# Norm work between the two halves of each softmax step in a two-layer transformer and mixture-of-experts kernel

## The chip, the cores and the metric

The kernel runs on one core of one Trainium2 chip. The metric is the time of one execution on the device, in microseconds (us); the median of three runs is given. Everything is float32.

## What is computed

Two blocks follow each other. The change touches only the first, a transformer of two layers (l = 0, 1) of width 1024 with 256 latent tokens (x) and 256 context tokens (h_ctx). Cut to what matters:

```python
def merge_heads(attn, sgu, four, g_mix, w_out):
    a = rmsnorm(attn, g_mix[:ATTN_WIDTH])
    s = rmsnorm(sgu, g_mix[ATTN_WIDTH:ATTN_WIDTH + SGU_WIDTH])
    f = rmsnorm(four, g_mix[ATTN_WIDTH + SGU_WIDTH:])
    return jnp.concatenate([a, s, f], axis=-1) @ w_out
...
    c_attn = context_attention(cq, ck, cv, sink[l])            # layer 0 only
    yc = merge_heads(c_attn, c_sgu, c_four, g_mix[l], w_out[l])
...
    attn = latent_window_attention(q, k, v, ck, cv, sink[l])
    sgu = spatial_gating(jax.nn.gelu(u), jax.nn.gelu(gv), w_sgu[l], b_sgu[l], g_sgu[l])
    four = fourier_mix(f)
    y = merge_heads(attn, sgu, four, g_mix[l], w_out[l])
    x = x + g1 * rmsnorm(y, g_post_mix[l])
```

Each attention is a softmax with a sink over 8 heads. After it comes a squared-relu MLP of width 4096. The second block is a recurrent unit, gated linear attention in chunks, and a mixture of 32 experts of which each token takes 4.

## The kernel before, in words

Each engine runs its own program, written out by hand, and the engines meet at semaphores. TensorE (PE) multiplies into eight PSUM banks. PE's program takes the banks in turn (`take`): each product, mean, transpose or score takes the next one and waits until its last user has been read. Two scores of a step take an even bank and the one behind it, so the turn may skip one (`F.even`).

Sides are called C (context) and X (latent tokens); an attention is a pair (layer, side). There are three: (0, C), (0, X) and (1, X). Each has eight units, a unit being two heads' scores for 128 queries, and PE's `attention(l, s, i)` in step i issues the scores of unit i+1, the transposes of unit i-1 and the value products of unit i-2:

```python
                if i + 1 < 8:
                    scores(l, s, i + 1)
                if 0 <= i - 1 < 8:
                    turned(l, s, i - 1)
                if 0 <= i - 2 < 8:
                    values(l, s, i - 2)
```

VectorE (DVE) does the softmax in two halves. `soft_a` adds the band mask (X only, L1878), takes the maximum (L1880) and from it and the sink the exponentials' bias (L1881, L1882) and the sink's exponent (L1884). ScalarE (ACT) makes the exponentials with their sums (L1362, L1365), which also frees the scores' banks. `soft_b` of the unit before adds sum and sink, takes the reciprocal and scales the probabilities (L1891, L1892, L1895). PE transposes them (L572), ScalarE reads the transposes out (L1271), PE multiplies by the values (L586), ScalarE reads the result into CAT (L1271).

The three parts of the joint output, Fourier (mF, tiles 6 and 7 of CAT), gating (mS, 4 and 5) and attention (mA, 0 to 3), are each normed by a root mean square. ScalarE squares the tiles (`merge_squares`, L1299), POOL adds the squares (L2443), PE's `merge` multiplies by a constant to make the mean (L470, and L473 for the fourth square of mA), VectorE reads the mean into HOLD (L1795), ScalarE makes the reciprocal root as exp(-ln/2) (`root`, L1304, L1306), VectorE refines it by a Newton step (L1797 to L1799, with L1795 the function `rstd`) and scales the tiles by gain and root (L1909, the function `merge`). After that PE may multiply CAT by w_out (L607), one output tile per `w_out(l, s, n)`; ScalarE's `joined` reads the tile and squares it (L1271, L1376).

Among the steps of (0, C) stand PE's projections of the latent tokens (`w_in`, L497 to L508), which ScalarE reads, four of them through gelu; the gelu table and that of exp and ln displace each other on ScalarE (ACT_TABLE_LOAD). Among the steps of (0, X) stand the output tiles 0 to 5 of (0, C). Among those of (1, X) stand four products of the modulation (`ada`, L448), whose row ScalarE copies (`row`, L1271), PE transposes (`ada_turn`, L456) and VectorE adds up (L1778, L1780). Weights of all these are chunks of 2 MB in a ring, loaded by the SyncE queue when PE is through with the slot's last chunk; from the experts on the ring has eight slots.

## Time and profile before

| | |
|---|---|
| median of 3 runs | 2451.59 us (2449.55 to 2455.35) |
| profiled execution, its own time | 2454.41 us |
| its span, first to last instruction | 2452.5 us |
| mean granted TensorE clock | 0.982 of full |
| busy PE, DVE, ACT, POOL | 2310.3, 806.9, 487.8, 136.8 us |
| DMA | 601.61 MB, 245 GB/s on average |

The profile is one execution. Busy time counts an engine's own instructions, not the time in which it waits or issues. A wait is put down to the engine or DMA whose signal came last. The granted clock is the share of full TensorE speed that the chip allowed in a stretch; its two levels are 1.2 and 2.4 GHz, so a stretch at 0.9 was partly at the lower one. The three attention stages lie at about 128 to 197 us, 209 to 278 us and 803 to 865 us of the span.

### The profile page before, as it was taken

What the parts mean: (1) busy time and instruction counts of PE and PEld (TensorE: products, weight loads), DVE (VectorE), ACT (ScalarE), POOL (GpSimd) and SP (SyncE); (2) the same over time, 40 slices, a digit from 0 to 9 for tenths busy, and PEclk for the clock granted to TensorE, in tenths of its full rate; (3) what the DMA queues carried; (4) which work ended last, traced back from release to release, by engine and by line L of the source; (5) the groups of instructions that cost most, each with busy time, mean ns of one, the idle gap of its engine ahead of it and who ended that gap; (6) DMA issues with size and microseconds to landing.
All of it is one profiled execution on the core that took longest, in us unless ns stands there. A gap on an engine that the chain in (4) does not pass through costs nothing.

```text
span 2452.5 us, 34141 instructions
## 1 busy us (share of the span) xinstructions
PE 2310.3 (94%) x14422; PEld 1687.5 (69%) x14422; DVE 806.9 (33%) x2047; ACT 487.8 (20%) x1144; POOL 136.8 (6%) x138
## 2 busy tenths in 40 slices
PE   6888999999999789999999989999999999999997
PEld 3675788888887468887778854566566555555556
DVE  2044354577714520001665321222222222222223
ACT  2244330000013432100534120111111111111112
POOL 0000211134400000000000000000000000000000
PEclk9999999999999999999999999999999999999999
DMA  8910222124323433445233575899999999999991
GB/s 337 354 69 35 94 78 103 69 103 145 131 96 149 167 137 137 142 167 199 105 137 137 216 301 212 364 427 427 426 425 427 426 427 426 426 427 427 427 426 78
DMA packets 42115, 601.61 MB, mean 245 GB/s; under 512 B 4672, under 2 KB 5184, under 8 KB 5600
## 3 DMA queue, kind: packets, MB, share of 16 engines
q1 hardware_dynamic: 41472, 593.30, 59.8%
q10 hardware_dynamic: 480, 5.97, 0.6%
q8 instruction: 122, 2.00, 0.3%
q14 instruction: 41, 0.34, 0.0%
HBM read 598.20 MB, written 1.05 MB: 244 GB/s over the span
## 4 chain that ended last, share of the span: by engine, by line
PE 81%; DMA 13%; DVE 2%; ACT 2%; issue 1%; POOL 0%; SPq 0%; POOLq 0%; PEldq 0%; ACTq 0%; DVEq 0%
PE PS L1095 14%; PE PS L854 7%; PE PS L1119 7%; DMA RG<-in_w_up 7%; PE PS L633 7%; PE PS L668 6%; PE PS L617 6%; PE PS L720 5%; DMA BIG<-in_w_up 4%; PE PS L508 4%; PE PS L607 3%; PE PS L706 2%; PE PS L1028 2%; PE PS L1131 2%; PE PS L564 2%; DMA RG<-in_w_ada 1%
## 5 line engine op out<-in xcount | busy, mean ns | idle before, releaser
L2318 DVE TENSOR_SCALAR STAT<-PS 128x128 f32<-128x128 f32 (+1 forms) x128 | 37.8, 296 | 683.1 <-PE PS L1095 683.1
L1095 PE MATMUL PS<-BIG,XS 128*64 128x256 f32 (+1 forms) x2016 | 239.8, 388 | 8.3 <-DMA BIG<-in_w_up 8.0
L1095 PEld LDWEIGHTS PS<-BIG,XS 128*64 128x64 f32 (+1 forms) x2016 | 146.4, 139 | 99.8 <-issue 20.4
L1095 PE MATMUL PS<-RG,XS 128*64 128x256 f32 (+1 forms) x1520 | 180.2, 387 | 10.1 <-DMA RG<-in_w_up 10.1
L1271 ACT ACTIVATE BIG<-PS 128x256 f32<-128x256 f32 (+2 forms) x205 | 86.5, 430 | 515.1 <-PE PS L633 138.9
L854 PE MATMUL PS<-XS,RG 128*128 128x256 f32 x768 | 172.1, 382 | 5.0 <-DVE XS L1822 4.1
L1095 PEld LDWEIGHTS PS<-RG,XS 128*64 128x64 f32 (+1 forms) x1520 | 108.9, 139 | 80.4 <-DMA RG<-in_w_up 15.9
L854 PEld LDWEIGHTS PS<-XS,RG 128*128 128x128 f32 x768 | 145.6, 191 | 26.7 <-issue 6.9
L1678 ACT ACTIVATE STAT<-STAT 128x128 f32<-128x128 f32 (+1 forms) x128 | 40.1, 313 | 585.5 <-DVE STAT L2318 585.5
L617 PE MATMUL PS<-HN,RG 128*128 128x256 f32 x640 | 140.3, 382 | 4.0 <-ACT HN L1316 4.0
L1795 DVE TENSOR_SCALAR HOLD<-PS 128x256 f32<-128x256 f32 x27 | 11.4, 423 | 401.6 <-PE PS L484 299.8
L617 PEld LDWEIGHTS PS<-HN,RG 128*128 128x128 f32 x640 | 122.4, 192 | 21.4 <-issue 4.6
L1119 PE MATMUL PS<-BIG,CAT 128*64 128x256 f32 (+1 forms) x992 | 120.9, 387 | 0.1
L720 PE MATMUL PS<-BIG,RG 128*128 128x256 f32 x512 | 110.7, 379 | 0.0
L508 PE MATMUL PS<-HN,RG 128*128 128x256 f32 x448 | 103.6, 387 | 5.6 <-ACT HN L1316 3.4
L720 PEld LDWEIGHTS PS<-BIG,RG 128*128 128x128 f32 x512 | 97.3, 190 | 13.2
L1119 PEld LDWEIGHTS PS<-BIG,CAT 128*64 128x64 f32 (+1 forms) x992 | 73.6, 139 | 42.5 <-issue 10.0
L508 PEld LDWEIGHTS PS<-HN,RG 128*128 128x128 f32 x448 | 85.6, 194 | 22.3 <-issue 7.6
L607 PE MATMUL PS<-CAT,RG 128*128 128x256 f32 x384 | 87.8, 388 | 0.3 <-DVE CAT L1909 0.3
L1119 PE MATMUL PS<-RG,CAT 128*64 128x256 f32 x768 | 86.4, 381 | 0.4 <-DVE CAT L2327 0.4
L2443 POOL TENSOR_TENSOR HN<-HN 128x256 f32<-128x256 f32 x60 | 45.9, 765 | 732.9 <-ACT HN L1299 315.2
L607 PEld LDWEIGHTS PS<-CAT,RG 128*128 128x128 f32 x384 | 74.0, 194 | 12.2 <-DVE CAT L1909 1.0
(347 smaller groups left out, 3310.3 us busy)
## 6 DMA issues: line engine op xcount, KB each, us to landing
BIG<-in_w_up SPq DMA_DIRECT2D x64, 2048.0 KB, 30.3
RG<-in_w_up SPq DMA_DIRECT2D x48, 2048.0 KB, 30.4
RG<-in_w_ff SPq DMA_DIRECT2D x32, 2048.0 KB, 8.1
BIG<-in_w_down SPq DMA_DIRECT2D x32, 2048.0 KB, 31.2
RG<-in_w_ada SPq DMA_DIRECT2D x24, 2048.0 KB, 8.9
RG<-in_w_down SPq DMA_DIRECT2D x24, 2048.0 KB, 34.2
RG<-in_w_in SPq DMA_DIRECT2D x23, 2048.0 KB, 8.0
SM<-in_w_up SPq DMA_DIRECT2D x16, 2048.0 KB, 30.6
```

The costliest lines, as they stand in the source:

```text
L508: m = pe.matmul(banks[b][:, 0:256], w[:, k, c0:c0 + 128], N[:, k, :], start=k == 0, stop=k == 7)
L564: pe.matmul(banks[b][:, 0:wd], Q[s][:, j, qb * 128:qb * 128 + 128], KZ[:, hf, 512 - wd:512], start=True, stop=True).then_inc(s_full[b], 1)
L607: m = pe.matmul(banks[b][:, 0:256], w[:, k, 128 * (n % 4):128 * (n % 4) + 128], own(CAT, s)[:, k, :], start=i == 0, stop=i == 7)
L617: m = pe.matmul(banks[b][:, 0:256], w[:, k, 128 * n:128 * n + 128], own(HN, s)[:, k, :], start=k == 0, stop=k == 7)
L633: m = pe.matmul(banks[b][:, 0:256], w[:, k, :], a[:, k, :], start=not first and k == 0, stop=k == 3, skip_group_check=True)
L668: return pe.matmul(banks[b[j]][:, 256 * half:256 * half + 256], w, a, start=first and half == 0, stop=last, skip_group_check=True)
L706: m = pe.matmul(banks[b[s, o]][:, 0:256], w[:, k, 128 * o:128 * o + 128], own(FFH, s)[:, 16 * h + k, :], start=h + k == 0, stop=h * 16 + k ...
L720: m = pe.matmul(banks[b][:, 0:256], w[:, k, :], own(FFH, s)[:, k, :], start=k == 0, stop=k == 31)
L854: m = pe.matmul(banks[b][:, 0:256], w[:, k, 128 * n:128 * n + 128], src[:, k, 0:256], start=k == 0, stop=k == 7)
L1095: i = pe.matmul(half_of(b, h, sides), Xg[:, k, 0:cap], w[:, k, h * wd:h * wd + wd], start=False, stop=k == 7)
L1119: m = pe.matmul(half_of(b, h, sides), T_[:, k, :], w[:, k, h * wd:h * wd + wd], start=k == 0, stop=k == 7)
L1271: i = act.activation(dst, banks[b][rows, part], fn)
```

## The change

The norm's pieces and some neighbours take other places in the steps. Nothing is computed otherwise, and each engine has the same instructions.

- On VectorE `rstd` is split into `mean_read` and `refined`, and `merge` ends with `scaled`. In the three attentions the pieces stand between `soft_a` and `soft_b` of a step, one step apart: mean in one, refinement in the next, scaling in the one after. For (0, C) these are steps 3 to 7 of the attention (i = 5 to 9 of the loop), for both X steps 3 to 7. The mA norm of (0, C), which stood ahead of `gated(0, X)`, is spread over steps 0 to 2 of (0, X).
- On PE the means of mF and mS stand ahead of the step's scores instead of behind its values, for X one step earlier by number (3 and 5, not 4 and 6). The mA mean of (0, C) moves from ahead of gating to behind the first scores of (0, X).
- On ScalarE `attention` is split into `exponentials` and `read_outs`; the roots stand between them, and so do the output tiles (`joined`, of one step later) and the modulation rows (`row`, which now reads the product of PE's step before instead of waiting for that of the same step).
- On VectorE `turned` stands between the halves, one step later.

The core of the diff (lines that only mirror these are left out):

```diff
@@ -750,23 +750,23 @@
                     scores(0, C, 0)
                 if 1 <= i <= 5:
                     rotate(0, i - 1)
-                if i >= 2:
-                    attention(0, C, i - 2)
                 if i == 5:
                     merge("mF", 0, C)
                 if i == 7:
                     merge("mS", 0, C)
+                if i >= 2:
+                    attention(0, C, i - 2)
             fourier_d(0, X)
-            merge("mA", 0, C)
             gating(0, X)
             fourier_t(0, X)
             scores(0, X, 0)
+            merge("mA", 0, C)
             for i in range(10):
+                if i == 3:
+                    merge("mF", 0, X)
+                if i == 5:
+                    merge("mS", 0, X)
                 attention(0, X, i)
-                if i == 4:
-                    merge("mF", 0, X)
-                if i == 6:
-                    merge("mS", 0, X)
                 if 2 <= i < 8:
                     w_out(0, C, i - 2)
             w_out(0, C, 6)
...
@@ -1349,7 +1349,7 @@
                 for j in range(2):
                     evac(own(CAT, s)[:, 6 + j, :], ("four", l, s, j))
-            def attention(l, s, i):
+            def exponentials(l, s, i):
                 wd = 512 if s == X else 256
                 if i < 8:
                     u, par = units(l, s) + i, i % 2
@@ -1363,6 +1363,9 @@
                                        accum_out=dn[:, hf:hf + 1]).then_inc(s_free[b], 1)
                     act.wait_ge(s_es, u + 1)
                     act.activation(es, nm, ACT.Exp).then_inc(s_ex, 1)
+
+            def read_outs(l, s, i):
+                wd = 512 if s == X else 256
                 if 0 <= i - 1 < 8:
                     for hf in range(2):
                         evac(PT[:, (i - 1) % 2, hf, 0:wd], ("t", l, s, i - 1, hf), part=slice(0, wd))
@@ -1452,26 +1455,30 @@
                     merge_squares("mF", 0, C)
                     merge_squares("mS", 0, C)
                 if i >= 2:
-                    attention(0, C, i - 2)
+                    exponentials(0, C, i - 2)
                 if i == 5:
                     root(("mF", 0, C), C, 0)
                 if i == 7:
                     root(("mS", 0, C), C, 1)
+                if i >= 2:
+                    read_outs(0, C, i - 2)
...
-            root(("mA", 0, C), C, 2)
             fourier_t(0, X)
             merge_squares("mF", 0, X)
             merge_squares("mS", 0, X)
             for i in range(10):
-                attention(0, X, i)
-                if i == 4:
+                exponentials(0, X, i)
+                if i == 0:
+                    root(("mA", 0, C), C, 2)
+                if i == 3:
                     root(("mF", 0, X), X, 0)
-                if i == 6:
+                if i == 5:
                     root(("mS", 0, X), X, 1)
-                if 2 <= i < 8:
-                    joined(0, C, i - 2)
+                if 3 <= i < 9:
+                    joined(0, C, i - 3)
+                read_outs(0, X, i)
...
             for i in range(10):
-                attention(1, X, i)
-                if i == 4:
+                exponentials(1, X, i)
+                if 1 <= i <= 4:
+                    row(1, 5 + i)
+                if i == 3:
                     root(("mF", 1, X), X, 0)
-                if i == 6:
+                if i == 5:
                     root(("mS", 1, X), X, 1)
-                if i <= 3:
-                    row(1, 6 + i)
+                read_outs(1, X, i)
...
-            def rstd(key, eps, s=0, slot=0):
+            def mean_read(key, eps, s=0):
+                b = full(("ms",) + key)
+                dve.tensor_scalar(HOLD[:, 256 * s:256 * s + 256], banks[b][:, 0:256], eps, None, ALU.add).then_inc(s_free[b], 1)
+
+            def refined(key, s=0, slot=0):
                 r, me, tm = stat(s, slot), HOLD[:, 256 * s:256 * s + 256], HOLD[:, 512 + 256 * s:768 + 256 * s]
-                b = full(("ms",) + key)
-                dve.tensor_scalar(me, banks[b][:, 0:256], eps, None, ALU.add).then_inc(s_free[b], 1)
                 dve.wait_ge(s_root, ROOT[key] + 1)
                 step(dve.tensor_tensor(tm, r, r, ALU.mult))
                 step(dve.scalar_tensor_tensor(tm, tm, -0.5, me, ALU.mult, ALU.mult))
                 step(dve.scalar_tensor_tensor(r, tm, 1.5, r, ALU.add, ALU.mult))
                 return r
+
+            def rstd(key, eps, s=0, slot=0):
+                mean_read(key, eps, s)
+                return refined(key, s, slot)
...
-            def attention(l, s, i):
-                if i < 8:
-                    soft_a(l, s, i)
-                if 0 <= i - 1 < 8:
-                    soft_b(l, s, i - 1)
+            SLOT = {"mF": 0, "mS": 1, "mA": 2}
+
+            def scaled(part, l, s, ks=None):
+                gm = s1(f"g_mix{l}")
+                for k in ks or PARTS[part]:
+                    ck = own(CAT, s)[:, k, :]
+                    dve.scalar_tensor_tensor(ck, ck, gm[:, k:k + 1], stat(s, SLOT[part]), ALU.mult, ALU.mult).then_inc(s_mt, 1)
 
             def merge(part, l, s):
-                slot = ("mF", "mS", "mA").index(part)
-                r = rstd((part, l, s), 1e-6, s, slot)
-                gm = s1(f"g_mix{l}")
-                for k in PARTS[part]:
-                    ck = own(CAT, s)[:, k, :]
-                    dve.scalar_tensor_tensor(ck, ck, gm[:, k:k + 1], r, ALU.mult, ALU.mult).then_inc(s_mt, 1)
+                rstd((part, l, s), 1e-6, s, SLOT[part])
+                scaled(part, l, s)
...
+                if 2 <= i < 10:
+                    soft_a(0, C, i - 2)
+                if i == 5:
+                    mean_read(("mF", 0, C), 1e-6, C)
+                if i == 6:
+                    refined(("mF", 0, C), C, 0)
+                if i == 7:
+                    scaled("mF", 0, C)
+                    mean_read(("mS", 0, C), 1e-6, C)
+                if i == 8:
+                    refined(("mS", 0, C), C, 1)
+                if i == 9:
+                    scaled("mS", 0, C)
+                if 3 <= i < 11:
+                    soft_b(0, C, i - 3)
                 if i <= 5:
                     rope(0, i - 1)
-                if i == 5:
-                    merge("mF", 0, C)
-                if i == 7:
-                    merge("mS", 0, C)
             value_norm(0, X)
-            merge("mA", 0, C)
             gated(0, X)
             for i in range(10):
-                attention(0, X, i)
+                if i < 8:
+                    soft_a(0, X, i)
+                if i == 0:
+                    mean_read(("mA", 0, C), 1e-6, C)
+                if i == 1:
+                    refined(("mA", 0, C), C, 2)
+                    scaled("mA", 0, C, (0, 1))
+                if i == 2:
+                    scaled("mA", 0, C, (2, 3))
+                if i == 3:
+                    mean_read(("mF", 0, X), 1e-6, X)
                 if i == 4:
-                    merge("mF", 0, X)
+                    refined(("mF", 0, X), X, 0)
+                if i == 5:
+                    scaled("mF", 0, X)
+                    mean_read(("mS", 0, X), 1e-6, X)
                 if i == 6:
-                    merge("mS", 0, X)
+                    refined(("mS", 0, X), X, 1)
+                if i == 7:
+                    scaled("mS", 0, X)
+                if 1 <= i < 9:
+                    soft_b(0, X, i - 1)
             merge("mA", 0, X)
             post("mix", 0, C)
             prenorm("ff", 0, C)
@@ -2084,13 +2121,23 @@
             value_norm(1, X)
             gated(1, X)
             for i in range(10):
-                attention(1, X, i)
+                if i < 8:
+                    soft_a(1, X, i)
+                if 2 <= i <= 5:
+                    turned(1, 4 + i)
+                if i == 3:
+                    mean_read(("mF", 1, X), 1e-6, X)
                 if i == 4:
-                    merge("mF", 1, X)
+                    refined(("mF", 1, X), X, 0)
+                if i == 5:
+                    scaled("mF", 1, X)
+                    mean_read(("mS", 1, X), 1e-6, X)
                 if i == 6:
-                    merge("mS", 1, X)
-                if 1 <= i <= 4:
-                    turned(1, 5 + i)
+                    refined(("mS", 1, X), X, 1)
+                if i == 7:
+                    scaled("mS", 1, X)
+                if 1 <= i < 9:
+                    soft_b(1, X, i - 1)
```

Where the rows stand now. VectorE in the middle of the attention (0, X), first before: `soft_b`, then the whole mF norm (L1795 to L1909), then the next `soft_a`.

```order
L1891 TENSOR_TENSOR MISC<-MISC 128x2
L1892 RECIPROCAL MISC<-MISC 128x2
L1895 TENSOR_SCALAR BIG<-BIG,MISC 128x512 x2
L1795 TENSOR_SCALAR HOLD<-PS 128x256
L1797 TENSOR_TENSOR HOLD<-STAT 128x256
L1798 SCALAR_TENSOR_TENSOR HOLD<-HOLD 128x256
L1799 SCALAR_TENSOR_TENSOR STAT<-HOLD,STAT 128x256
L1909 SCALAR_TENSOR_TENSOR CAT<-CAT,SM,STAT 128x256 x2
L1878 TENSOR_TENSOR PS<-PS,SM 128x2x128
L1880 TENSOR_REDUCE MISC<-PS 128x2
L1881 SCALAR_TENSOR_TENSOR MISC<-MISC,SM 128x2
L1882 TENSOR_SCALAR MISC<-MISC 128x2
```

The same place in the changed kernel, where `mean_read` is L1802, `refined` L1807 to L1809, `soft_a` L1892 to L1898 and `soft_b` L1905 to L1909:

```order
L1802 TENSOR_SCALAR HOLD<-PS 128x256
L1905 TENSOR_TENSOR MISC<-MISC 128x2
L1906 RECIPROCAL MISC<-MISC 128x2
L1909 TENSOR_SCALAR BIG<-BIG,MISC 128x512 x2
L1892 TENSOR_TENSOR PS<-PS,SM 128x2x128
L1894 TENSOR_REDUCE MISC<-PS 128x2
L1895 SCALAR_TENSOR_TENSOR MISC<-MISC,SM 128x2
L1896 TENSOR_SCALAR MISC<-MISC 128x2
L1898 TENSOR_TENSOR MISC<-SM,MISC 128x2
L1807 TENSOR_TENSOR HOLD<-STAT 128x256
L1808 SCALAR_TENSOR_TENSOR HOLD<-HOLD 128x256
L1809 SCALAR_TENSOR_TENSOR STAT<-HOLD,STAT 128x256
```

The mean's read has moved ahead of a `soft_b`, the three refining instructions have a whole `soft_b` and `soft_a` between themselves and the read, and the scaling follows a step later.

PE between the attentions (0, C) and (0, X), as a piece of the difference (L523 is the first Fourier product, L546 gating, L534 the second Fourier product):

```order
@@ -86,6 +86,4 @@
 L586 MATMUL PS<-BIG 64x128 x4
 L523 MATMUL PS<-SM,BIG 128x256 x4
-L470 MATMUL PS<-HN,MISC 128x256
-L473 MATMUL PS<-HN,MISC 128x256
 L546 MATMUL PS<-SM,BIG 64x128 x8
 L534 MATMUL PS<-SM,BIG 128x256
```

The two matmuls of the mA mean are gone from ahead of gating. They come back behind the first scores (L564) of the next attention:

```order
@@ -97,6 +95,14 @@
 L534 MATMUL PS<-SM,BIG 128x256
 L535 MATMUL PS<-SM,BIG 128x256
-L564 MATMUL PS<-BIG 128x512 x6
+L564 MATMUL PS<-BIG 128x512 x2
+L470 MATMUL PS<-HN,MISC 128x256
+L473 MATMUL PS<-HN,MISC 128x256
+L564 MATMUL PS<-BIG 128x512 x4
 L572 MATMUL PS<-SM,BIG 128x128 x8
```

ScalarE in the attention (1, X), first before: the modulation row (L1271, SM) stands behind the read-outs and ahead of the next exponentials (L1362).

```order
L1271 ACTIVATE BIG<-PS 128x512 x2
L1271 ACTIVATE SM<-PS 128x512
L1362 ACTIVATE BIG,MISC<-PS,MISC 128x512 x2
L1365 ACTIVATE MISC<-MISC 128x2
L1271 ACTIVATE BIG<-PS 128x512 x2
L1271 ACTIVATE CAT<-PS 128x128
L1271 ACTIVATE SM<-PS 128x512
```

Now it stands right behind the exponentials, and the root (L1304, L1306) too:

```order
L1271 ACTIVATE BIG<-PS 128x512 x2
L1271 ACTIVATE CAT<-PS 128x128
L1362 ACTIVATE BIG,MISC<-PS,MISC 128x512 x2
L1365 ACTIVATE MISC<-MISC 128x2
L1271 ACTIVATE SM<-PS 128x512
L1304 ACTIVATE STAT<-HOLD 128x256
L1306 ACTIVATE STAT<-STAT 128x256
L1271 ACTIVATE BIG<-PS 128x512 x2
```

The read-outs of transposes (BIG) and values (CAT) now come last in a step.

## Rows read from the trace of the kernel before

**Rows 1.** The page, parts 1 and 4: busy time; chain that ended last
```profile
PE 2310.3 (94%) x14422; PEld 1687.5 (69%) x14422; DVE 806.9 (33%) x2047; ACT 487.8 (20%) x1144; POOL 136.8 (6%) x138
...
PE 81%; DMA 13%; DVE 2%; ACT 2%; issue 1%; POOL 0%; SPq 0%; POOLq 0%; PEldq 0%; ACTq 0%; DVEq 0%
```

**Rows 2.** Windows: length, busy PE, PEld, DVE, ACT, POOL (counts), clock, DMA share, GB/s
```profile
152.37:192.84 40.47, 32.16 (x155) 24.92 (x153) 15.52 (x51) 22.65 (x51) 0.00 (x0) 0.87 0.15 53
...
209.43:223.07 13.64, 11.61 (x49) 6.24 (x47) 10.22 (x26) 8.49 (x24) 1.45 (x2) 0.87 0.00 0
223.07:277.61 54.54, 47.92 (x278) 35.39 (x276) 20.81 (x59) 22.55 (x60) 3.62 (x5) 0.91 0.11 40
...
802.53:833.28 30.75, 27.68 (x185) 13.67 (x184) 17.33 (x51) 15.83 (x43) 1.72 (x2) 1.00 0.71 262
833.28:867.77 34.49, 18.44 (x127) 12.93 (x126) 16.44 (x47) 13.33 (x36) 1.44 (x2) 0.80 0.03 11
```

**Rows 3.** Waits of PE, 127 to 210: total us, times, longest
```profile
PE PS L564 <- ACT BIG L1362: 4.9, 2, 2.4
PE PS L470 <- POOLq L2446: 3.1, 1, 3.1
```

**Rows 4.** Waits of PE, 209 to 288, same columns
```profile
PE PS L572 <- DVE BIG L1895: 5.4, 2, 3.3
```

**Rows 5.** Waits of PE, 802 to 873, same columns
```profile
PE PS L564 <- ACT BIG L1362: 9.6, 3, 6.5
PE PS L572 <- DVE BIG L1895: 6.8, 1, 6.8
PE PS L470 <- POOLq L2446: 2.8, 1, 2.8
```

**Rows 6.** Timeline, DVE, B: start, length, line, tiles, [idle before]
```profile
238.99 0.42 DVE L1795 TENSOR_SCALAR HOLD<-PS 128x256 f32<-128x256 f32 x1 [6.96 <-PE PS L470]
240.34 0.42 DVE L1797 TENSOR_TENSOR HOLD<-STAT 128x256 f32<-128x256 f32 x1 [0.93 <-ACT STAT L1306]
...
241.72 0.88 DVE L1909 SCALAR_TENSOR_TENSOR CAT<-CAT,SM,STAT 128x256 f32<-128x256 f32 x2
242.52 0.43 DVE L1878 TENSOR_TENSOR PS<-PS,SM 128x256 f32<-128x256 f32 x1
```

**Rows 7.** Timeline, PE, B: scores after the norm of step 4
```profile
245.56 3.75 PE L564 MATMUL PS<-BIG 128*128 128x512 f32 x4 [3.16 <-ACT BIG L1362]
```

**Rows 8.** Timeline, PE, B: scores, transposes, output tile, next scores
```profile
226.63 1.88 PE L564 MATMUL PS<-BIG 128*128 128x512 f32 x4
228.38 1.32 PE L572 MATMUL PS<-SM,BIG 128*128 128x128 f32 x8
...
230.66 3.72 PE L607 MATMUL PS<-CAT,RG 128*128 128x256 f32 x16
234.22 1.88 PE L564 MATMUL PS<-BIG 128*128 128x512 f32 x4
```

**Rows 9.** Timeline, PE, C: transposes, later scores
```profile
815.09 1.04 PE L572 MATMUL PS<-SM,BIG 128*128 128x128 f32 x8
...
821.13 1.96 PE L564 MATMUL PS<-BIG 128*128 128x512 f32 x4 [1.54 <-ACT BIG L1362]
```

**Rows 10.** Timeline, start of B: DVE soft_a(1), soft_b(0); PE first transposes
```profile
213.55 0.43 DVE L1878 TENSOR_TENSOR PS<-PS,SM 128x256 f32<-128x256 f32 x1
...
215.75 0.15 DVE L1891 TENSOR_TENSOR MISC<-MISC 128x2 f32<-128x2 f32 x1
...
216.78 1.52 PE L572 MATMUL PS<-SM,BIG 128*128 128x128 f32 x8 [2.03 <-DVE BIG L1895]
```

**Rows 11.** Timeline, ACT, A: table load ahead of exponentials
```profile
156.42 1.28 ACT L1309 ACT_TABLE_LOAD   x1
```

**Rows 12.** Timeline, ACT, C: read-out of a modulation row
```profile
819.72 0.60 ACT L1271 ACTIVATE SM<-PS 128x512 f32<-128x512 f32 x1 [2.24 <-PE PS L448]
```

**Rows 13.** Windows, experts, columns as in rows 2
```profile
1560.00:1878.00 318.00, 316.77 (x2770) 193.14 (x2766) 71.60 (x257) 35.91 (x90) 0.00 (x0) 1.00 1.01 427
```

10 lines of the change are left out of this document (4 added, 6 removed).

## The prediction

> **What bounds the kernel now.** I read the page first: TensorE (PE) is busy for 94% of the span and carries 81% of the chain that ended last [rows 1]. A step that is moved is worth something only where PE stands still or runs slowly, so I cut the span at the three attention stages with the view by windows [rows 2]. Stage A (context tokens of layer 0, among the input projections of the latent tokens) has 8.3 us of idle PE in 40.5; the start of stage B (latent tokens, layer 0) 2.0 in 13.6; B's steady steps 6.6 in 54.5; stage C (layer 1) 3.1 in 30.8 and then 16.1 in 34.5. The clock column tells the rest: 0.80 to 0.91 where PE idles, 1.00 where it doesn't. I write the lower clock's cost as excess: busy time above what the same matmuls take at the full level.
>
> The waits say who is late. In A: the scores' banks, freed by ScalarE's exponentials; in the passage from A to B 3.1 us for the POOL sums of the attention part's norm [rows 3]. In B: transposes that wait for VectorE's scaled probabilities [rows 4], and once scores that wait for exponentials. In C the same two, longer, and the POOL sum again [rows 5]. The timeline of B shows how that comes about. PE makes the norm's mean; VectorE reads it at 238.99, then stands still for 0.93 us until ScalarE has made the root, refines it, scales two tiles and only at 242.52 begins the next softmax, whose scores had been ready [rows 6]. ScalarE's exponentials are late by as much, and PE's next scores find their bank occupied: 3.16 us idle, and the scores then take 3.75 us at the lower of the two clock levels (1.2 GHz), against 1.88 at 2.4 GHz [rows 7, 8].
>
> **Stage B, steady steps.** The change gives the norm's mean, refinement and scaling to three different steps, behind the maximum of a softmax (soft_a) and ahead of the normalisation of the one before (soft_b); PE makes the mean ahead of the scores of its step. VectorE then never waits for the root: ScalarE makes it one step earlier. What is added ahead of soft_b is 0.42 us (mean), 1.4 (three refining instructions, 240.34 to 241.72) or 0.84 (two tiles) [rows 6]. A step on PE lasts 7.6 us from one output tile to the next [rows 8]; VectorE's own work in it is 2.2 for soft_a (213.55 to 215.75) and 1.2 for soft_b (1.03 from its start to the first transposes, and the second tile) [rows 10], so up to 1.4 more still leaves it 2.8 us early. ScalarE reads output tile n one step later than before, so the exponentials no longer stand behind a tile that PE ends last in the step. The banks turn in the same eight; I followed each take and found one place in B where a wait remains, about 0.4 us for the last values. PE's work at the full level: six output tiles at 3.56 (230.66 to 234.22) are 21.4, four scores at 1.75 (226.63 to 228.38) are 7.0, six transposes at 1.0 are 6.0, seven values at 1.0 are 7.0, two means 1.1 [rows 8, 9]. That is 42.5, with the wait 42.9, against 54.5: **11.6 us**. Lower end: only the 6.6 idle goes and the excess stays; upper end 12.
>
> **Passage and start of B.** The attention part's mean is moved from ahead of gating to behind the first scores. The 3.1 us wait for POOL [rows 3] is then covered by gating and the Fourier products, save that gating itself waits for VectorE's value norm, which ends about when PE gets there; with the mean's own matmuls out of the way gating starts 3.3 us earlier. But VectorE had done this norm behind gating and Fourier, in nobody's way. Now it stands in the start of the softmax: read 0.42, refinement 1.4, two of the four tiles 0.84, together 2.66, all ahead of soft_b(0). The first transpose, which came right on the heels of that soft_b [rows 10], comes 2.6 us later after its scores. What is left is 3.3 - 2.6 = **0.7 us**. The other two tiles stand ahead of soft_b(1) and are hidden by the scores that PE has in between. PE now stands still for about 3.7 us in one piece at the first transpose, where it stood 2.0, and the clock in that window was already 0.87 [rows 2], so I keep its excess as it was. The Trainium skill (TensorE: Matmul & The Clock Gate, What's actually happening) says that the throttled state is the default and that sustained activity releases it; by that rule the longer idle piece speaks against this change and would cost some 2 us more at the start, a sum of 26.5 in place of 28.5. The trace agrees as far as the slow scores behind the 3.16 us wait go [rows 7]; no row shows this very place. Ends: -2 to +3.
>
> **Stage A.** From step 6 on each step waits for one chain: projection, gelu read-out, table load 1.28 us [rows 11], exponentials. The order of these isn't touched, so these waits stay; the softmax that was late through the norm in steps 6 and 8 was covered by this chain in any case. Two things change. The scores now mostly find a bank that isn't the previous scores' one, so PE does 0.9 us of scores before it waits and meets the wait at the transpose; and the mean of step 5 fills a wait of 0.6. Against that soft_b(2) comes 0.3 late behind the mean's read. Walking steps 5 to 10 gives 7.9 us of waits where there were 8.3 and half a microsecond less in step 5: **0.7 us**. Ends: -1.5; +6 if the excess (0.13 of 40.5, so 5.3) went too.
>
> **Stage C.** Here the read-out of a modulation row stood at the end of ScalarE's step, behind PE's last product; the next exponentials stood behind it [rows 12], and PE's scores waited 1.54 twice [rows 9]. It now stands between exponentials and read-outs and reads the product of the step before. With the two norms (6.5 and 6.8 us of idle, most of [rows 5]) treated as in B, PE's work is: eight scores 14.4, eight transposes 8.0, eight values 8.1, four row products 7.4, four turns 2.4, two means 1.1, together 41.4. Waits that I still find: 0.3 at the scores of step 5, 1.1 at the transpose of step 6, 2.2 at that of step 7 (no row products fill these steps, and VectorE's 2.2 + 0.84 + 1.2 is longer than PE's work), 0.3, and the POOL sum's 2.8, which isn't touched. That is 48.1, and 1.6 for the clock behind the waits: 49.7 against 65.2, **15.5 us**. Lower end 9 (a microsecond or two of wait in each of four steps and half the excess kept), upper end 17.
>
> No instruction is added or taken away, no DMA is moved in its queue, and the weights' slots come free relative to PE as before. **Sum:** 0.7 + 0.7 + 11.6 + 15.5 = 28.5. Is it kept to the end? From 1560 us on, the experts' weights stream at 427 GB/s without a gap [rows 13], and later PE waits for them (most of the 13% of DMA in the chain [rows 1]). But this stream can only start when PE gives back the slots of the first experts, after everything above; it moves forward with PE. The profiled execution took 2454.41 us; less 28.5 it is 2425.9. The median of the runs is 2.8 below the profiled one, so the forecast for the median is **2423 us**.
>
> **Rivals.**
> First, half of it: the moved pieces stand ahead of soft_b, and a mean must have come from PE before soft_b may run. If each norm step costs a microsecond of wait for VectorE and the excess stays in B and C, B gives 6.6, C 10, the rest nothing: 2451.6 - 16.6 = 2435. For it: VectorE's margin comes from hand-walked steps, and in C it is gone from step 6 on. Against: in B the margin is 2.8 us in steps of 7.3.
> Second, nothing arrives: the weight stream bounds the end and the gain ends as waiting for it, 2451.6. For it: the stream is saturated [rows 13]. Against: its start is tied to PE.
> Third, slower, through the clock. New short waits at the transposes, one in most steps, with the 3.7 us at B's start could hold PE at the 1.2 GHz level across steps that ran at 2.4. B and C hold 42.5 + 41.4 = 83.9 us of work at the full level, which doubles at the lower one; once more than a third of it (28.5) runs there, the gain is gone. Half of it there gives 2423 + 42 = 2465. For it: A shows 0.87 with waits of about 2 us in each step. Against: B keeps almost no wait, and C's first half shows 1.00 with two waits of 1.5. The rule of the Trainium skill cited above would work through this mechanism.
>
> **How the numbers follow.** The forecast with its bounds 0.72, half 0.20, nothing 0.03, slower 0.03, and 0.02 for a gain above the upper ends. All lower ends together give 12, all upper ones 38; both at once are unlikely. From 2414 to 2438 holds the forecast's spread and most of the half case. A measurement of this kernel tells about 0.2%, 5 us, from no change: faster 0.94, within it 0.03, slower 0.03.
>
> **What would show it.** In the profile after: B's steady part near 43 us with clock near 1.00 and no idle PE behind L1362 or soft_b; C near 50; the POOL wait of the passage gone and a wait of 3 to 4 us at B's first transpose in its place; A unchanged within 2. VectorE's 0.93 us wait for the root is gone in B and C, and the stream's full rate starts some 28 us earlier. Wrong would be: scores that still wait for exponentials in B, the clock of B below 0.95, or soft_b behind a mean that PE hasn't made.

## The result, and the profile of the changed kernel

| | before | changed |
|---|---|---|
| median | 2452.80 us (4 runs, 2449.55 to 2455.35) | 2423.02 us (4 runs, 2419.32 to 2425.50) |
| ratio, 95% interval | | 0.9884, 0.9872 to 0.9896 |
| profiled execution: own time, span | 2454.41, 2452.5 us | 2425.50, 2423.6 us |
| mean granted TensorE clock | 0.982 | 0.983 |

The forecast was 2423 us. Its sum was made against the profiled execution and gave 2425.9 for it; 2425.5 was measured. Two executions, one of the kernel before (11141.6 us, granted clock 0.202) and one of the sums alone below (3473.11 us, 0.651), are left out of everything below. The terms did not all come out as well as their sum, so I take them one by one. The cuts are starts of PE instructions, the same in every kernel. A: first scores of (0, C) to the first Fourier product. Passage: from there to the first scores of (0, X). Start of B: from there to the first output tile. B: first to seventh output tile. C: first scores of (1, X) to the mean of its attention part.

| us | before | changed | gained | predicted |
|---|---|---|---|---|
| A | 69.45 | 66.43 | 3.0 | 0.7 |
| passage + start of B | 12.35 + 13.64 | 7.43 + 17.45 | 1.1 | 0.7 |
| B, steady steps | 54.54 | 42.20 | 12.3 | 11.6 |
| C | 65.25 | 49.07 | 16.2 | 15.5 |
| all the rest, code unchanged | 2237.3 | 2241.0 | -3.7 | 0 |

The last line is a surprise: the same instructions lasted 3.7 us longer. It is taken up below. Each column is one execution, and the other kernels' profiles show that the lengths of A, of the passage, of the start, of B and of C also differ from one execution to the next; the part on the prediction gives each gain with that spread.

Windows of the changed kernel. In order: A, the start of B, B, C up to the end of the scores of step 5, the rest of C, and the same stretch of the experts as in [rows 13]. Columns as in [rows 2].

```profile
129.31:195.74 66.43, 59.34 (x320) 47.84 (x318) 30.44 (x99) 32.17 (x88) 1.97 (x2) 0.95 0.18 64
203.17:220.62 17.45, 13.74 (x54) 7.91 (x52) 13.77 (x36) 9.11 (x26) 1.45 (x2) 0.80 0.00 0
220.62:262.82 42.20, 42.11 (x278) 33.16 (x277) 20.38 (x57) 21.80 (x60) 3.63 (x5) 1.00 0.15 51
789.42:820.17 30.75, 30.59 (x194) 15.05 (x193) 23.57 (x69) 18.85 (x52) 1.72 (x2) 1.00 0.73 271
820.17:838.49 18.32, 12.69 (x118) 9.80 (x117) 9.97 (x30) 9.91 (x27) 1.44 (x2) 0.91 0.02 6
1560.00:1878.00 318.00, 316.77 (x2772) 192.93 (x2770) 72.63 (x261) 36.21 (x91) 0.00 (x0) 1.00 1.01 426
```

The third line, against that of [rows 2] which begins at 223.07, is the core of the change. PE was busy for 47.92 of 54.54 us at 0.91 and is now busy for 42.11 of 42.20 at 1.00: 6.5 us of idle time and 5.8 of excess are gone. Not all of the excess was the clock: a clock of 0.91 over 54.54 us is some 5 us lost, idle time included. The experts' stream is as dense as in [rows 13]. It starts earlier with PE: from the first expert product to the end it is 1017.25 us, against 1016.97.

Waits of PE in the changed kernel, 203 to 275 us:

```profile
PE PS L572 <- DVE BIG L1909: 3.7, 1, 3.7
PE PS L484 <- ACT HN L1379: 0.5, 1, 0.5
```

The same view, 789 to 850 us, to be held against [rows 5]:

```profile
PE PS L572 <- DVE BIG L1909: 2.8, 2, 2.1
PE PS L470 <- POOLq L2493: 2.8, 1, 2.8
PE PS L607 <- DVE CAT L1917: 1.6, 1, 1.6
PE PS L564 <- ACT BIG L1362: 0.2, 1, 0.2
```

No wait is left in B's steps. What is left at its start is the 3.7 us that the prediction put there. C's list is the predicted one, a little shorter, and one more: 1.6 at the first output tile.

VectorE in B, one norm spread over three steps:

```profile
224.81 0.42 DVE L1802 TENSOR_SCALAR HOLD<-PS 128x256 f32<-128x256 f32 x1 [4.07 <-PE PS L470]
225.15 0.15 DVE L1905 TENSOR_TENSOR MISC<-MISC 128x2 f32<-128x2 f32 x1
...
228.73 0.42 DVE L1807 TENSOR_TENSOR HOLD<-STAT 128x256 f32<-128x256 f32 x1
...
233.79 0.43 DVE L1892 TENSOR_TENSOR PS<-PS,SM 128x256 f32<-128x256 f32 x1 [2.42 <-PE PS L564]
...
235.99 0.87 DVE L1917 SCALAR_TENSOR_TENSOR CAT<-CAT,SM,STAT 128x256 f32<-128x256 f32 x2
```

The 0.93 us wait for the root of [rows 6] is gone: the mean is read at 224.81, the refinement comes 3.9 us later. VectorE now waits for scores (2.42), where PE's scores used to wait behind it [rows 7].

PE in the changed kernel, the start of B and two steps:

```profile
213.06 1.94 PE L572 MATMUL PS<-SM,BIG 128*128 128x128 f32 x8 [3.71 <-DVE BIG L1909]
214.79 3.62 PE L564 MATMUL PS<-BIG 128*128 128x512 f32 x4
...
226.32 1.04 PE L572 MATMUL PS<-SM,BIG 128*128 128x128 f32 x8
227.29 1.09 PE L586 MATMUL PS<-BIG 128*64 128x128 f32 x16
228.32 3.72 PE L607 MATMUL PS<-CAT,RG 128*128 128x256 f32 x16
231.87 1.88 PE L564 MATMUL PS<-BIG 128*128 128x512 f32 x4
```

From one step's transposes to the next step's it is now 7.3 us, with PE busy throughout. The scores at 214.79 take twice the 1.88 of those at 231.87: behind the 3.71 us of idle time PE is at the lower clock level for a while.

### The profile page after: what moved, and what is told of

It reads as the page before. It is cut to its first block, busy times and chain, and to the rows that moved or that the text cites. A ratio compares the mean times of both kernels' runs of the same rounds, so it can differ in the third digit from the quotient of the medians.

```text
span 2423.6 us, 34147 instructions
## 1 busy us (share of the span) xinstructions
PE 2301.6 (95%) x14422; PEld 1683.5 (69%) x14422; DVE 806.4 (33%) x2047; ACT 486.2 (20%) x1144; POOL 136.9 (6%) x138
## 4 chain that ended last, share of the span: by engine, by line
PE 81%; DMA 13%; DVE 2%; ACT 2%; issue 1%; POOL 0%; SPq 0%; POOLq 0%; PEldq 0%; ACTq 0%; DVEq 0%
PE PS L1095 14%; PE PS L854 8%; PE PS L1119 7%; DMA RG<-in_w_up 7%; PE PS L633 7%; PE PS L668 6%; PE PS L617 6%; PE PS L720 5%; DMA BIG<-in_w_up 4%; PE PS L508 4%; PE PS L607 3%; PE PS L706 2%; PE PS L1028 2%; PE PS L1131 2%; PE PS L448 1%; DMA RG<-in_w_ada 1%
## 5 line engine op out<-in xcount | busy, mean ns | idle before, releaser
L1095 PE MATMUL PS<-BIG,XS 128*64 128x256 f32 (+1 forms) x2016 | 239.9, 388 | 8.4 <-DMA BIG<-in_w_up 8.3
L1095 PEld LDWEIGHTS PS<-BIG,XS 128*64 128x64 f32 (+1 forms) x2016 | 146.7, 139 | 99.7 <-issue 20.5
L1095 PE MATMUL PS<-RG,XS 128*64 128x256 f32 (+1 forms) x1520 | 181.0, 388 | 9.8 <-DMA RG<-in_w_up 9.8
L1271 ACT ACTIVATE BIG<-PS 128x256 f32<-128x256 f32 (+2 forms) x205 | 85.9, 430 | 508.4 <-PE PS L633 138.9
L1095 PEld LDWEIGHTS PS<-RG,XS 128*64 128x64 f32 (+1 forms) x1520 | 109.1, 139 | 80.2 <-issue 16.1
L1802 DVE TENSOR_SCALAR HOLD<-PS 128x256 f32<-128x256 f32 x27 | 11.4, 423 | 383.7 <-PE PS L484 299.9
```

Source lines behind the costliest of these rows:

```text
L1095: i = pe.matmul(half_of(b, h, sides), Xg[:, k, 0:cap], w[:, k, h * wd:h * wd + wd], start=False, stop=k == 7)
L1271: i = act.activation(dst, banks[b][rows, part], fn)
```

## The experiments

Each kernel was run beside the kernel before on the same chip; its segments are cut as above. "The change" is the changed kernel. Line numbers differ from kernel to kernel.

### The parts one by one

Each stage's part of the diff was put into the kernel before on its own. First **C alone**: all hunks for (1, X) on the three engines, of which this is PE's.

```diff
             for i in range(10):
+                if i == 3:
+                    merge("mF", 1, X)
+                if i == 5:
+                    merge("mS", 1, X)
                 attention(1, X, i)
-                if i == 4:
-                    merge("mF", 1, X)
-                if i == 6:
-                    merge("mS", 1, X)
```

> The kernel before with the change in the attention (1, X) alone. If the gain of each stage is its own waits (theory), stage C takes 49 us instead of 65 and the whole is about 16 us (0.66%) faster than before; A, passage and B are as before. If the gain came from the clock recovering over the whole first block, C alone would keep part of its waits' excess and give under 10 us.

2433.64 us, ratio 0.9934 (0.9917 to 0.9950), C 47.52 us at a clock of 1.00. The gain is C's own, as expected. **B alone**, the same hunks for (0, X) with the output tiles on ScalarE, without the mA norm of (0, C):

```diff
-                if 2 <= i < 8:
-                    joined(0, C, i - 2)
+                if 3 <= i < 9:
+                    joined(0, C, i - 3)
+                read_outs(0, X, i)
```

> The kernel before with the change in the steps of the attention (0, X) alone; the mA norm of (0, C) and stage C stay. Theory: the steady part of B 42 to 43 us instead of 54.5, its start 13.6 as before, about 12 us (0.49%) faster. Rival (clock): with the slow clock of stage A in front, the steady part would stay above 46.

2441.56 us, ratio 0.9961 (0.9951 to 0.9971), B 42.21 us, so the clock in front of it doesn't hold it up. **A alone**, the hunks for (0, C):

```diff
-                if i >= 2:
-                    attention(0, C, i - 2)
                 if i == 5:
                     merge("mF", 0, C)
                 if i == 7:
                     merge("mS", 0, C)
+                if i >= 2:
+                    attention(0, C, i - 2)
```

> The kernel before, with the change made in the steps of (0, C) alone. Theory: A's gain of the change (3.0 us by the segment where 0.7 was predicted) is one of its own: A 66.4 or 64.9 in place of 69.5, B and C as before (54.5 and 65.3), 3 us faster by the span, some 2449. Rival: A's length differs between executions by steps of about 1.5 us whatever the kernel, and half of the gain is such a step; then A here comes out at 67.9 and the time at 2450.5.

2448.26 us, ratio 0.9987 (0.9977 to 0.9997), A 66.43 us, to the hundredth the length that it has in the change. The three ratios fall short of 1 by 0.66%, 0.39% and 0.13%, together 1.18%; the change falls short by 1.16%. So the parts add up as far as the intervals tell (together about 0.2%, 5 us), and what is moved between A and B (the mA norm) is worth no more than that. The prediction's 0.7 for A was too small.

Windows of A, first of the kernel before, then of A alone:

```profile
127.63:197.08 69.45, 60.56 (x320) 49.08 (x318) 30.54 (x99) 32.35 (x88) 1.97 (x2) 0.93 0.17 61
```

```profile
126.48:192.91 66.43, 59.33 (x321) 47.84 (x319) 30.46 (x99) 32.16 (x88) 1.97 (x2) 0.95 0.18 64
```

Idle time went from 8.9 to 7.1 us, busy time from 60.6 to 59.3: 1.8 and 1.2 us. The idle time is a property of the code: it is 8.9 in all six profiles whose code of A is that of the kernel before, and 7.1 in all eight with the change. The busy time is not: A took 69.5 us in three of the six and 67.7 to 67.9 in the other three, and 66.4 in three of the eight and 64.9 in five.

### The attention part's norm at the start of B

The change with the mA norm of (0, C) where it was before:

```diff
             fourier_d(0, X)
+            merge("mA", 0, C)
             gating(0, X)
             fourier_t(0, X)
             scores(0, X, 0)
-            merge("mA", 0, C)
```

> The changed kernel with the mA norm of (0, C) put back on all three engines: ahead of gating. Theory: passage 12.3 us (7.4 in the change) and B's start 13.6 (17.5), so about 1 us slower than the change, that is nearly the same: what the passage gains the start gives back. Rival: moving the norm was a clear part of the gain, 3 us or more.

2423.81 us, ratio 0.9884 (0.9868 to 0.9901), the same as the change. The passage is 12.33, the start of B 13.63 us, as before, with the waits that were there before. Its waits from 195 to 225 us:

```profile
PE PS L470 <- POOLq L2486: 3.1, 1, 3.1
PE PS L572 <- DVE BIG L1908: 2.0, 1, 2.0
```

Against this profile the passage of the change gains 4.9, and its start gives back 3.8. Both numbers hold a piece of clock that belongs to the execution. Here are the passage and the start in C alone, which has the norm in the same place:

```profile
195.24:205.96 10.72, 7.61 (x46) 6.11 (x45) 5.33 (x14) 4.21 (x12) 1.45 (x2) 1.00 0.55 196
205.96:218.71 12.75, 10.12 (x50) 5.31 (x48) 11.66 (x30) 8.51 (x24) 1.56 (x2) 1.00 0.00 0
```

The wait for POOL is the same 3.1 us, and yet the passage takes 10.72 in place of 12.35 us. B alone and the three kernels below that move the row, the sums or both have the same two lengths.

Then the change with only the mean's read ahead of `soft_b`, refinement and scaling behind it (VectorE, (0, X)):

```diff
                 if i == 0:
                     mean_read(("mA", 0, C), 1e-6, C)
-                if i == 1:
-                    refined(("mA", 0, C), C, 2)
-                    scaled("mA", 0, C, (0, 1))
-                if i == 2:
-                    scaled("mA", 0, C, (2, 3))
...
                 if 1 <= i < 9:
                     soft_b(0, X, i - 1)
+                if i == 1:
+                    refined(("mA", 0, C), C, 2)
+                if i == 2:
+                    scaled("mA", 0, C)
```

> The changed kernel with the refinement and the scaling of the mA norm of (0, C) behind soft_b of steps 1 and 2 instead of ahead of it; its mean's read stays. Theory: the 3.7 us wait of the first transpose falls to about 1.5, B's start takes 14 to 15 us instead of 17.5, the whole is about 3 us faster than the change. Rival (PE's start is bound by the scores and the exponentials, not by soft_b): start stays at 17.

2421.42 us, ratio 0.9886 (0.9869 to 0.9902), not told from the change. Start of B 15.48 us, where 14 to 15 were expected. PE's timeline of this kernel says why:

```profile
207.31 1.06 PE L572 MATMUL PS<-SM,BIG 128*128 128x128 f32 x8 [1.54 <-DVE BIG L1909]
212.07 1.17 PE L572 MATMUL PS<-SM,BIG 128*128 128x128 f32 x8 [1.98 <-DVE BIG L1909]
```

The first wait is 2.2 us shorter, as expected, but the second transposes now wait 1.98: the refinement behind `soft_b(0)` delays the next `soft_a`. Together they are 3.5 us, only 0.2 less than before the move; most of the difference to 17.45 is the clock (0.93 in this window, 0.80 in the change's), and other profiles of the change's code at this place show 16.09. VectorE has little room at this start (busy for 13.77 us of 17.45 in the change's second window above), so a piece that is moved off one wait lands in the next.

### "Between the halves" or "a step apart"?

The change does two things at once. **In one piece**: the whole norm stands between the halves, in one step (both X):

```diff
                 if i == 3:
-                    mean_read(("mF", 0, X), 1e-6, X)
-                if i == 4:
-                    refined(("mF", 0, X), X, 0)
+                    merge("mF", 0, X)
                 if i == 5:
-                    scaled("mF", 0, X)
-                    mean_read(("mS", 0, X), 1e-6, X)
-                if i == 6:
-                    refined(("mS", 0, X), X, 1)
-                if i == 7:
-                    scaled("mS", 0, X)
+                    merge("mS", 0, X)
```

> The changed kernel, but in both X attentions VectorE does mean, wait for the root, refinement and scaling of mF in step 3 and of mS in step 5 in one piece, ahead of soft_b. Theory (what counts is that VectorE doesn't wait for the root with a softmax behind it): about 3 us more per norm in B and for mF in C, so steady part of B 48 us, C 52, about 9 us slower than the change. Rival (PE's and ScalarE's new order does it all): B and C within 1 us of the change.

2435.52 us (2 runs), ratio 0.9926 (0.9897 to 0.9954); B 50.33, C 54.84, both 2 to 3 us more than expected. VectorE and then PE in B:

```profile
222.65 0.42 DVE L1807 TENSOR_TENSOR HOLD<-STAT 128x256 f32<-128x256 f32 x1 [0.93 <-ACT STAT L1306]
```

```profile
225.84 1.06 PE L572 MATMUL PS<-SM,BIG 128*128 128x128 f32 x8 [2.88 <-DVE BIG L1909]
...
244.29 1.59 PE L572 MATMUL PS<-SM,BIG 128*128 128x128 f32 x8 [3.30 <-DVE BIG L1909]
```

The 0.93 us for the root is back, the norm's 3.6 us (0.42 + 0.93 + 1.4 + 0.84) stand in one piece ahead of the scaled probabilities, and PE pays twice. The run doesn't tell the wait for the root from the 2.7 us of work that now also stand in one step; no run splits the work but keeps the wait, or the other way round. **Behind `soft_b`**: the pieces a step apart as in the change, but all behind `soft_b`:

```diff
+                if 1 <= i < 9:
+                    soft_b(0, X, i - 1)
                 if i == 3:
                     mean_read(("mF", 0, X), 1e-6, X)
...
                 if i == 7:
                     scaled("mS", 0, X)
-                if 1 <= i < 9:
-                    soft_b(0, X, i - 1)
```

> The changed kernel with the pieces still a step apart, but behind soft_b instead of between the halves. Theory: a step apart is what counts; B unchanged at 42.2 us, C 0.5 to 1.5 us shorter, since the transposes of steps 6 and 7 no longer wait for refinement and scaling. Rival (between the halves is what counts): B and C each 2 us or more longer.

2424.51 us (2 runs), ratio 0.9881 (0.9852 to 0.9910); B 42.20, C 46.75. Its waits from 784 to 846 us:

```profile
PE PS L470 <- POOLq L2493: 2.8, 1, 2.8
PE PS L572 <- DVE BIG L1909: 2.3, 1, 2.3
PE PS L564 <- ACT BIG L1362: 0.2, 1, 0.2
```

In whole times as fast as the change, to within the 0.3% of the interval. In B the idle time of PE is 6.6 us in the kernel before, 6.3 in one piece and 0.1 a step apart, on either side of `soft_b`: there the spacing of the pieces is what gains, and the rest of the new order gives next to nothing without it. In C it is one of three gains. The idle time is 19.1 us in the kernel before, 15.8 with rows and sums moved (both, below), 9.8 in one piece, 5.8 in the change and 5.3 behind `soft_b`. Besides rows and sums, the step to 9.8 holds PE's earlier means, ScalarE's new order and the place between the halves, which no run takes apart in C.

### The output tiles

The change with ScalarE's read-out of output tile n back at the end of its own step:

```diff
                 if i == 5:
                     root(("mS", 0, X), X, 1)
-                if 3 <= i < 9:
-                    joined(0, C, i - 3)
                 read_outs(0, X, i)
+                if 2 <= i < 8:
+                    joined(0, C, i - 2)
```

> The changed kernel with the output tiles' read-out on ScalarE back at the end of the step that makes the tile. Theory: the exponentials stand behind it again and the second bank of the scores is freed late: 0.1 to 0.3 us in each of some five steps, steady part of B 43 to 44 us instead of 42.2. Rival: no difference, since VectorE's soft_b ends later anyway.

B 46.62 us, 4.4 more than in the change and more than the 43 to 44 expected. PE's timeline, and the window of B:

```profile
220.26 1.95 PE L564 MATMUL PS<-BIG 128*128 128x512 f32 x4 [1.25 <-ACT BIG L1362]
...
237.03 1.96 PE L564 MATMUL PS<-BIG 128*128 128x512 f32 x4 [1.25 <-ACT BIG L1362]
...
253.71 1.09 PE L586 MATMUL PS<-BIG 128*64 128x128 f32 x16 [0.72 <-ACT BIG L1362]
```

```profile
214.85:261.47 46.62, 43.29 (x278) 32.80 (x276) 21.00 (x59) 21.71 (x60) 3.63 (x5) 1.00 0.13 46
```

The exponentials stand behind a tile that PE ends last in the step. Of the 4.4 us, 3.2 are these waits. The other 1.2 are busy time (43.29 us, where the same matmuls take 42.11 in the change) and not the clock, which is at 1.00 throughout; two groups of transposes last 1.33 us in place of 1.04, and the rest stays open. Two runs of the whole kernel (2426.56 us, ratio 0.9889, 0.9860 to 0.9918) do not tell it from the change; the segment does.

### The two waits of 1.5 us in C's first half

The prediction gave them to ScalarE's read-out of the modulation row alone. Into the kernel before went first only that move, **the row alone**:

```diff
                 exponentials(1, X, i)
+                if 1 <= i <= 4:
+                    row(1, 5 + i)
                 read_outs(1, X, i)
...
-                if i <= 3:
-                    row(1, 6 + i)
```

> The kernel before, with only the modulation rows of stage C on ScalarE moved from the end of the step to behind the exponentials, and so reading the product of the step before. Theory: the two waits of 1.54 us of the scores go and nothing else, stage C 62 us instead of 65.2. Rival: the waits are the exponentials' own and stay.

2450.95 us, ratio 0.9998 (0.9986 to 1.0010). The expectation failed: both waits stayed, at 1.53 us each. VectorE in this kernel:

```profile
813.50 0.19 DVE L1784 TENSOR_REDUCE MODT<-PS 128x8 f32<-128x32 f32 x1 [2.48 <-PE PS L456]
813.72 0.17 DVE L1786 TENSOR_TENSOR MODT<-MODT,SM 128x8 f32<-128x8 f32 x1
813.80 0.43 DVE L1890 TENSOR_TENSOR PS<-PS,SM 128x256 f32<-128x256 f32 x1
```

The sums of the turned row (the function `turned`, the first two rows) stand ahead of the next `soft_a` (the third) and wait for PE's turn, which comes late in the step. The scores were ready meanwhile. The change had moved these sums as well, and the prediction names them nowhere. So **the sums alone** and **both**:

```diff
                 if i < 8:
                     soft_a(1, X, i)
+                if 2 <= i <= 5:
+                    turned(1, 4 + i)
...
-                if 1 <= i <= 4:
-                    turned(1, 5 + i)
```

> The kernel before, with VectorE's sums of the turned row alone moved behind soft_a, a step later; ScalarE's row stays at the end of the step. Theory that both stand in the way (ScalarE's row waits for PE's last product of the step and holds the next exponentials, VectorE's sums hold soft_a): the waits of 1.5 us stay, at most a few tenths shorter, C 64.5 to 65.3. Theory that VectorE alone was in the way: they go, C 62 to 63.

2450.68 us (9 runs), ratio 1.0003 (0.9993 to 1.0013), both waits at 1.54. ScalarE in this kernel: the row waits for PE's last product, and the exponentials behind it start at 814.47, although VectorE's bias for them was ready at 811.6.

```profile
813.97 0.60 ACT L1271 ACTIVATE SM<-PS 128x512 f32<-128x512 f32 x1 [2.24 <-PE PS L448]
814.47 0.68 ACT L1362 ACTIVATE BIG<-PS,MISC 128x512 f32<-128x512 f32 x1
815.04 0.20 ACT L1362 ACTIVATION_READ_ACCUMULATOR BIG<-PS,MISC 128x1 f32 x1
```

> The kernel before, with the modulation row's read-out moved behind the exponentials and VectorE's sums of the turned row moved behind soft_a, a step later (in (1, X) only; norms and everything else as before). Theory: the two waits of 1.5 us in C's first half came from VectorE, which stood behind PE's turn at the end of a step and so began soft_a late; they go, C is 62 to 63 in place of 65.3, the rest unchanged: 2.5 to 3 us faster, some 2448.5. Rival (the row on ScalarE alone, as the prediction had it): already refuted by the row alone; then C would stay at 65. If both are needed, neither alone gives anything, and this one does.

2446.43 us (10 runs), ratio 0.9984 (0.9974 to 0.9995). C is 61.83 and the two waits are gone; ScalarE's row now waits behind the exponentials:

```profile
812.36 0.69 ACT L1362 ACTIVATE BIG<-PS,MISC 128x512 f32<-128x512 f32 x1
...
814.66 0.60 ACT L1271 ACTIVATE SM<-PS 128x512 f32<-128x512 f32 x1 [0.76 <-PE PS L448]
```

Neither move alone gives anything, both together 3.4 us of C: two engines were late by the same amount for the same scores, each hidden by the other.

### A version that takes the remaining waits too

The change, with refinement and scaling of the mA norm of (0, C) and of the mS norm of (1, X) behind `soft_b`, and C's output tiles begun with the four tiles of CAT that are ready. PE:

```diff
+            w_out_first(1, X, 0)
+            w_out_first(1, X, 1)
             merge("mA", 1, X)
-            for n in range(8):
+            w_out_first(1, X, 2)
+            for n in range(3):
+                w_out_rest(1, X, n)
+            for n in range(3, 8):
                 w_out(1, X, n)
```

> The change, and besides: refinement and scaling of the mA norm of (0, C) behind soft_b of steps 1 and 2; in (1, X) refinement and scaling of the mS norm behind soft_b of steps 6 and 8; and the products with w_out of the first three output tiles of (1, X) begun with the four tiles of CAT that are ready, two of them ahead of the mA mean and one behind it, finished when the attention's tiles are scaled. Theory: start of B 1 to 2 us shorter (15.5 in place of 17.5), C's steps 1 to 2 shorter, and the waits of 2.8 (POOL's sum) and 1.6 (VectorE's scaling) at C's end filled with 5.3 us of matmuls that were due anyway: another 3 to 4. Together 5 to 7 us faster than the change, some 2417. Rival (the waits' place is taken by the lower clock or by the next wait of VectorE, the root of mA): 1 to 3 us, some 2421.

2419.56 us (4 runs), ratio 0.9857 (0.9835 to 0.9879). PE at C's end in this kernel:

```profile
830.14 3.72 PE L606 MATMUL PS<-CAT,RG 128*128 128x256 f32 x16
833.70 0.59 PE L470 MATMUL PS<-HN,MISC 128*128 128x256 f32 x2
...
834.56 1.89 PE L606 MATMUL PS<-CAT,RG 128*128 128x256 f32 x8
838.03 5.45 PE L614 MATMUL PS<-CAT,RG 128*128 128x256 f32 x24 [1.58 <-DVE CAT L1939]
```

The 2.8 us wait for POOL is filled. The 1.58 for VectorE's scaling stays: it follows the mean, wherever the mean stands. From C's first scores to the mean of the joint squares (L482) it is 75.9 us; 79.5 in the change, 77.9 in the kernel with the mA norm behind `soft_b`, whose code of C is the change's own, and 77.3 in the one with all pieces behind it. So this end gains 2.0 to 3.6 us over the change, by the execution, and 1.4 over that one; 3 to 4 from filling and 1 to 2 from the steps were expected. The whole kernel's interval overlaps the change's, so it is the fastest median here but not shown to be faster.

## Why the prediction was right

**B, 11.6 predicted, 12.3 measured.** Every step held: the means one step ahead, no wait for the root, no scores behind a tile, 42.20 us where 42.9 were built up from durations. The 0.4 us wait that I had found did not show. The experiment with the output tiles bears out that they are part of it. One reservation: B in the kernel before is not always 54.54. In the row alone and the sums alone, which don't touch it, it was 51.69 and 51.68, with the same 6.6 us of idle time and a clock of 0.97; in A alone, C alone and both it was 54.5. With the change it is 42.2 in four profiles. B alone brought 0.39% (0.29 to 0.49), which is 9.6 us. The gain lies between 9.5 and 12.3, by the execution. A second reservation: the prediction read the excess as the clock alone. Of its 5.8 us the clock accounts for some 5 at most; the rest is something else, as in the experiment with the output tiles.

**C, 15.5 predicted, 16.2 measured.** The predicted waits 0.3, 1.1, 2.2, 0.3 and 2.8 came as 0.16, 0.76, 2.08, none and 2.79, and its 41.4 us of work as 41.7 in C alone, at a clock of 1.00. The 1.6 for the clock is an affair of the execution: 1.5 in the change's profile, nothing in C alone and in the kernel with the mA norm behind `soft_b`, where C is 47.52. So the gain is 16.2 to 17.7. The step that fails is the attribution of the two waits of 1.54: "It now stands between exponentials and read-outs" is true of ScalarE's row, but the row alone gives nothing. VectorE's sums had to be moved too. The sum came out since it was built from PE's work with all waits taken out, not from the reasons for them. The 1.6 at the first output tile lies behind the cut of C, and was 0.3 before. PE does 8 matmuls ahead of it, in 1.89 us now; before, at the lower level, in 3.15, which covered the difference.

**A, 0.7 predicted, 3.0 measured.** Mis-sized twice. Idle time fell by 1.8 us, where the prediction's own terms give 0.4 + 0.5: the wait of step 5 went from 0.59 to 0.15, two waits of 2.44 at the scores became waits of 1.49 at the transposes, and one of 1.49 became 2.01. The clock term, which I had left at zero, is 1.2 between these two profiles. By the lengths given under A alone the gain is anywhere from 1.3 to 4.6 us between two executions, and 2.8 to 3.1 between the longer lengths of each kind as well as between the shorter ones; A alone brought 0.13% (0.03 to 0.23), 3.2 us. That it belongs to this part is settled, its clock share is not.

**Passage and start of B, 3.3 - 2.6 = 0.7 predicted, 4.9 - 3.8 = 1.1 measured.** The first transposes came 9.9 us behind the first scores instead of 7.35 (209.43 to 216.78): 2.5 later, as predicted. The rest of the difference is the clock, and mostly the execution's. Where the old passage ran at 1.00 it took 10.72 us with the same wait, so at the full level the passage gains 3.3, the predicted number, and the further 1.6 is not the change's doing. The start of B took 13.64 us in three profiles without the change and 12.75 in the five others (C alone and those named with it); with it, it took 17.45 or 16.09. Together passage and start are 26.0 or 23.5 us before and 24.9 or 23.5 with the change. The gain lies between -1.4 and 2.5 us, and no run tells it from nothing. What the prediction left out is the clock at the start: of the 13.74 us busy in the change's window 0.9 are the mean's own matmuls, so the lower level costs 1.3 us more than in the kernel before (11.61 busy), and 2.8 more than in a start at 1.00 (10.12 busy); where the start is 16.09 (12.4 busy) it is 1.4. That is the place at which the prediction weighed the Trainium skill (TensorE: Matmul & The Clock Gate, What's actually happening), by whose rule the throttled state is the default and sustained activity releases it. The trace agrees: behind the 3.71 us of idle time the scores take 3.62 us in place of 1.88, and the cost, 1.3 to 2.8 us, is about the 2 that the prediction had estimated and then kept out of its sum.

**The rivals.** Half: the windows of B and C exclude it. Nothing arrives: excluded, the experts' stream starts 29 us earlier. Slower through the clock: B ran at 1.00 throughout, and only its start lost something to the lower level. None of them had more part in the result. The clock column doesn't follow idle time as neatly as the prediction's first paragraph has it (1.00 where PE doesn't idle): its own row of C's first half has 3.1 us of idle time at 1.00.

**The -3.7 us in unchanged code.** Of it 1.7 lie ahead of A and 1.7 between B and C. In the other kernels, whose code there is the same, A begins anywhere from 126.4 to 131.9 us, and from the first matmul of L633 in layer 0 to C it is either 453.04 to 453.12 or 454.61 to 454.75 us. So this is the execution, not the change. The sum of my errors (+2.3, +0.4, +0.7, +0.7) and this loss nearly cancelled; the hit within 0.4 us is partly luck.

## What to carry to other kernels

A chain that crosses engines (mean, root, refinement, scaling) can hold up the whole pipeline if it stands in one piece, and costs nothing if each link stands one step behind the one it needs and the step has room for it: in B 6.3 us of idle time against 0.1. In C, whose last steps are too short for VectorE's work, 2.8 us stayed. On which side of `soft_b` the links stand mattered little, nothing in B and 0.5 us in C. Before a wait is given to one instruction, ask of every engine on the way what stands ahead of its next piece: two that are late by the same time hide each other, and only the move of both shows. Once the waits are gone, count the clock as well, and count it as a range: in B the time gained beyond the idle time was 3.0 to 5.8 us, by the execution, more than half of it the clock.

## What the hardware showed unexpectedly

A stage of unchanged code does not have one length. PE's stretches at the lower clock level begin and end at different points in different executions, and some are missing in some: the passage ran at 0.86 or at 1.00 behind the same wait. Around the first expert product the same matmuls behind the same waits took this in the version with the mA norm behind `soft_b`:

```profile
1396.37:1407.50 11.13, 9.76 (x89) 5.34 (x84) 2.58 (x10) 2.92 (x5) 0.00 (x0) 1.00 0.26 82
```

and this in the last version:

```profile
1396.10:1412.70 16.60, 15.23 (x92) 7.33 (x88) 2.66 (x10) 2.91 (x5) 0.00 (x0) 0.64 0.17 58
```

Idle time is 1.37 us in both, the clock 1.00 against 0.64; from the mean at L482 of layer 1 to the first expert product (L1095) that makes 541.8 instead of 537.5 us. Elsewhere the steps are 1.4 to 1.8 us (A 66.43 or 64.90 and C 49.07 or 47.52 in the changed code, the passage 12.35 or 10.72 in the old), once 2.9 (B of the kernel before, 54.54 or 51.69). The kernel before spreads over 2448.3 to 2455.4 us from run to run. So a difference of 2 or 3 us between two profiled executions says nothing by itself: a segment must be compared with the same segment of kernels that leave it alone, and times with several runs. What sets the point at which the level rises was not tried.
